# A two-stage transformer on one core: attention heads in another order, a bias mask on GpSimd, and other slots for VectorE's work

## The reference

```python
proj = rms_norm(x, pre_mix_norm[l]) @ w_in[l]
a_out = neighbourhood_attention(na_q, na_k, na_v, na_rel_bias[l])    # bias table and window mask
b_out = diff_attention(dq1, dq2, dk1, dk2, df_v, lam, alibi_slopes)  # 4 heads, two softmaxes each
b_out = rms_norm(b_out, diff_subln[l]) * (1.0 - lambda_init)         # norm over each head's 64 columns
c_out = gqa_attention(rope(norm(gq_q)), rope(norm(gq_k)), gq_v)
d_out = mla_attention(q_nope, q_rope, k_nope, k_rope, v)
x = x + rms_norm(concat(a_out, b_out, c_out, d_out) @ w_o[l], post_mix_norm[l])
x = x + rms_norm(ffn(rms_norm(x)), post_ffn_norm[l])                 # SwiGLU, 2816 wide
```

## Time and profile before

| what | value |
|---|---|
| time, median of 3 runs (lowest to highest) | 1947.78 us (1947.43 to 1951.02) |
| the profiled execution: its time, its span | 1951.02 us, 1949.2 us |
| TensorE busy, mean granted clock | 1883.7 us (97%), 0.989 |
| VectorE, ScalarE, GpSimd busy | 1343.0 us (69%), 995.4 us (51%), 68.5 us (4%) |
| shares of the chain that ended last | PE 81%, DVE 9%, ACT 4% |

### The profile page before, as it was taken

One profiled execution on the slowest core, in us unless ns is written; L12 is line 12 of the kernel. 1 busy time (PEld: TensorE's weight loads), 2 busy tenths in 40 slices (PEclk: granted clock), 3 DMA queues, 4 the chain that ended last, 5 costly groups with the idle time before them and its releaser, 6 DMA issues.

```text
span 1949.2 us, 34518 instructions
## 1 busy us (share of the span) xinstructions
PE 1883.7 (97%) x13470; PEld 1730.1 (89%) x13470; DVE 1343.0 (69%) x2141; ACT 995.4 (51%) x1534; POOL 68.5 (4%) x82
## 2 busy tenths in 40 slices
PE   8999999999999999999999999998999999999998
PEld 7978999898899987899989799998989998979997
DVE  5757888675788876788878578885555555665555
ACT  7755333765533466633374453346655335655333
POOL 3002000000000000000000000003300000000000
PEclk9999999999999999999999999999999999999999
DMA  8527988532788842588853368874335554325552
GB/s 288 191 90 238 359 311 311 185 130 89 286 316 314 310 149 94 212 323 311 314 193 130 132 247 322 313 292 171 141 114 200 183 185 171 111 85 179 188 194 86
DMA packets 60355, 412.22 MB, mean 211 GB/s; under 512 B 8592, under 2 KB 8784, under 8 KB 11616
## 3 DMA queue, kind: packets, MB, share of 16 engines
q1 hardware_dynamic: 55728, 401.33, 55.7%
q0 software_dynamic: 4528, 9.56, 1.8%
HBM read 409.71 MB, written 3.16 MB: 212 GB/s over the span
## 4 chain that ended last, share of the span: by engine, by line
PE 81%; DVE 9%; ACT 4%; DVEq 2%; issue 2%; ACTq 1%; DMA 0%; SPq 0%
PE psu L502 33%; PE psy L661 16%; PE psy L564 6%; PE psy L610 5%; PE psy L556 4%; PE psm L736 3%; PE psu L519 3%; PE psu L721 2%; DVE wlo L855 2%; PE psy L632 2%; PE psy L543 1%; PE pso L707 1%; DVE ada_raw L1017 1%; DVE x L1084 1%; ACT whi L846 1%
## 5 line engine op out<-in xcount | busy, mean ns | idle before, releaser
L846 ACT CAST whi<-raw 128x2048 fp32r<-128x2048 f32 (+1 forms) x281 | 536.2, 1908 | 624.6 <-PE psu L502 424.3
L855 DVE TENSOR_TENSOR wlo<-raw,whi 128x2048 fp32r<-128x2048 f32 (+5 forms) x296 | 645.4, 2181 | 276.4 <-ACT whi L846 275.0
L502 PE MATMUL psu<-hhi,whi 128*128 128x256 f32 x1920 | 537.0, 280 | 0.0
L502 PE MATMUL psu<-hlo,whi 128*128 128x256 f32 x1920 | 535.9, 279 | 0.0
L502 PE MATMUL psu<-hhi,wlo 128*128 128x256 f32 x1920 | 535.8, 279 | 0.0
L502 PEld LDWEIGHTS psu<-hhi,whi 128*128 128x128 f32 x1920 | 360.8, 188 | 3.0
L502 PEld LDWEIGHTS psu<-hlo,whi 128*128 128x128 f32 x1920 | 360.8, 188 | 2.4
L502 PEld LDWEIGHTS psu<-hhi,wlo 128*128 128x128 f32 x1920 | 360.8, 188 | 0.0
L1017 DVE CUSTOM_DVE_ANT_0 ada_raw<-ada_raw,cvec 128x1024 f32<-128x1024 f32 x192 | 227.0, 1219 | 1.3 <-DMA ada_raw<-ada 1.2
L661 PE MATMUL psy<-whi,ahi 128*128 128x512 f32 x528 | 210.5, 399 | 1.0 <-DVE alo L1036 0.9
L661 PE MATMUL psy<-wlo,ahi 128*128 128x512 f32 x528 | 208.0, 394 | 0.0
(11 more groups left out here) (342 smaller groups left out, 3055.2 us busy)
## 6 DMA issues: line engine op xcount, KB each, us to landing
raw<-wts SPq DMA_DIRECT2D x280, 1024.0 KB, 4.8
ada_raw<-ada SPq DMA_DIRECT2D x96, 1024.0 KB, 4.8
dense_bias<-rel_bias POOLq DMA_DIRECT2D x32, 64.0 KB, 12.5
nab<-dense_bias SPq DMA_DIRECT2D x2, 1024.0 KB, 7.6
ada_raw<-fox_rows POOLq DMA_DIRECT2D x4, 512.0 KB, 6.8
cb<-cst POOLq DMA_DIRECT2D x1, 1408.0 KB, 8.5
cb<-cst SPq DMA_DIRECT2D x1, 1056.0 KB, 10.6
x<-x_in SPq DMA_DIRECT2D x2, 512.0 KB, 4.7
```

Source lines behind the costliest of these rows:

```text
L502: last = mm(psu[:, bank, cc * SEQ:(cc + 1) * SEQ], a[:, cols], h[:, kt, :], start=(kt == 0 and j == 0), stop=(kt == KT - 1 and j == 2))
L846: nc.scalar.copy(whi[:, part_of(c), 0:n], raw[:, slot_of(c), 0:n]).then_inc(hi_done, 1)
L855: last = nc.vector.tensor_tensor(wlo[:, part_of(c), cols], raw[:, slot_of(c), cols], whi[:, part_of(c), cols].bitcast(f32), ALU.subtract)
```

## The change

1. MIX: the items' order is gqa, diff, na, mla. The result's columns, the rows of `w_o` and the turns are permuted to fit: turns 0 and 1 (gqa) go to slots 17 and 19, and turns 2 and 3 (diff) at 28 and 29 wait for `mix_ready`. `sub_sums` goes from slot 22 to 26, the square root with its table changes from 22 to 27, `sub_norm` from 23 to 27.
2. MIX: the queries' transposes for gqa go to the bank `psy[:, 2]` (was `psu[:, 1]`).
3. MIX: `neighbour_mask` is gone from VectorE; GpSimd adds the mask in one instruction over 128x2048, as soon as the bias table has landed. The na items wait for it (`na_ready`).
4. FOX: GpSimd adds the columns by eight `tensor_scalar` per group (four 128x128, four 128x256) with drains, in place of three `tensor_tensor` with a broadcast column.
5. GLA: the second half of the ada step goes from slot 40 to 7; `take_level(0)` from slot 16 to 17; the `dve_lo` that stood at slot 16 behind it is at slot 15. All other entries of `GLA.lo` stay as they were.

```diff
@@ -79,14 +79,13 @@
...
 MIX = Plan([2 if u is None else 4 for u in W_IN1], [3, 3, 2] + [2] * 11 + [1] * 20 + [2] * 4, range(12, 32),
-           [24, 25, 28, 29, 30, 31, 33, 35], "00 01 10 02 03 11 12 13",
+           [17, 19, 28, 29, 30, 31, 33, 35], "00 01 10 02 03 11 12 13",
            [2, 3, 5, 7, 10, 11, 13, 14, 18, 22, 26, 30, 34], 24)
...
            "00 01 10 02 03 11 12 13", [2, 4, 6, 8, 13, 17, 20, 24], 16)
-GLA = Plan([4] * 13, [3, 4, 1] + [1] * 60, [], [45, 46, 49, 50, 52, 53, 55, 57], "00 10 01 11 02 12 03 13",
-           [2, 3, 7, 11, 16] + list(range(19, 63, 4)))
+GLA = Plan([4] * 13, [3, 4, 1] + [1] * 60, [], [45, 46, 49, 50, 52, 53, 55, 57], "00 10 01 11 02 12 03 13")
 GLA_LEVEL = {16: 0, 18: 1, 22: 2, 26: 3, 30: 4, 34: 5, 38: 6}
...
@@ -242,6 +241,7 @@
...
+        na_ready = sem("na_ready")
...
@@ -282,7 +282,6 @@
...
-        fox_sum = sem("fox_sum")
...
@@ -455,6 +454,11 @@
...
                 pool.dma_start(gain[:], gain_mix[l].partition_broadcast(P)).then_inc(gain_loaded, 16)
+                pool.wait_ge(na_loaded, 16 * (l + 1))
+                pool.wait_ge(cb1_loaded, 16)
+                nb = fold(nab[:], 32, 64)
+                mask = cb[:, CB1["na"][0]:CB1["na"][1]]
+                nc.gpsimd.tensor_tensor(nb, nb, mask.unsqueeze(1).to_broadcast([P, 32, 64]), ALU.add).then_inc(na_ready, 1)
                 pool.wait_ge(x_ready, 8 + 8 * l)
...
@@ -475,11 +479,14 @@
...
                 first = fold(nab[:, g4 * 512:(g4 + 1) * 512], 4, P)
-                own, later = (lcq[:, at + 4 * g4:at + 4 * g4 + 4].unsqueeze(2).to_broadcast([P, 4, P]) for at in (0, 16))
-                nc.gpsimd.tensor_tensor(first, rows4[:, :, 0:P], own, ALU.add)
-                nc.gpsimd.tensor_tensor(rows4[:, :, P:], rows4[:, :, P:], later, ALU.add).then_inc(fox_sum, 1)
-                pool.wait_ge(fox_sum, g4 + 1)
-                nc.gpsimd.tensor_tensor(rows4[:, :, 0:P], rows4[:, :, 0:P], later, ALU.add)
+                for i in range(4):
+                    h = 4 * g4 + i
+                    nc.gpsimd.tensor_scalar(first[:, i], rows4[:, i, 0:P], lcq[:, h:h + 1], None, ALU.add)
+                nc.gpsimd.drain()
+                for i in range(4):
+                    h = 4 * g4 + i
+                    nc.gpsimd.tensor_scalar(rows4[:, i], rows4[:, i], lcq[:, 16 + h:17 + h], None, ALU.add)
+                nc.gpsimd.drain()
                 nc.gpsimd.tensor_tensor(first, first, mask, ALU.add)
...
@@ -750,10 +757,10 @@
...
             if m is not None:
-                if m < 2:
+                if m in (2, 3):
                     pe.wait_ge(mix_ready, l + 1)
                 else:
-                    pe.wait_ge(o_evac, I0 + 2 * m + 6)
+                    pe.wait_ge(o_evac, I0 + (2 * m + 2 if m < 2 else 2 * m + 6))
                 pe_turn(pe, l, m)
...
@@ -1116,26 +1123,26 @@
...
                                     [gv[:, kc * P + kv * HD:kc * P + (kv + 1) * HD] for kc in range(2)],
-                                    256 + (2 * c + kv) * HD, pre=(gqa_ready, l + 1), vpre=(bank_free, b0 + 4)))
+                                    (2 * c + kv) * HD, pre=(gqa_ready, l + 1), vpre=(bank_free, b0 + 4)))
             for h in range(4):
...
                                     [dfv[:, kc * 256 + h * HD:kc * 256 + (h + 1) * HD] for kc in range(2)],
-                                    h * HD, table=distance_table, slope=2.0 ** (-8.0 * (h + 1) / 4), pair=which,
+                                    256 + h * HD, table=distance_table, slope=2.0 ** (-8.0 * (h + 1) / 4), pair=which,
                                     pre=(bank_free, b0 + 6), vpre=(bank_free, b0 + 7)))
...
                                 [nav[:, kc * 256 + h * HD:kc * 256 + (h + 1) * HD] for kc in range(2)],
-                                512 + h * HD, table=na_table(h),
+                                512 + h * HD, table=na_table(h), tpre=(na_ready, l + 1),
                                 pre=(bank_free, b0 + 9), vpre=(bank_free, b0 + 10)))
...
                                 768 + h * HD, pre=(ml_cev, 4 * l + 4), vpre=(ml_evac, l + 1)))
-            return out[4:12] + out[0:4] + out[12:]
+            return out
 
...
@@ -1195,7 +1202,7 @@
...
                         for k in range(2):
-                            nc.tensor.transpose(psu[:, 1, k * SEQ + t * P:k * SEQ + (t + 1) * P],
+                            nc.tensor.transpose(psy[:, 2, k * SEQ + t * P:k * SEQ + (t + 1) * P],
                                                 gqr[:, t * 256 + k * P:t * 256 + (k + 1) * P], ident[:])
...
@@ -1279,13 +1286,13 @@
...
                     act.wait_ge(gq_tr, l + 1)
-                    nc.scalar.activation(gqT, psu[:, 1], ACT.Copy, scale=HD ** -0.5)
+                    nc.scalar.activation(gqT, psy[:, 2], ACT.Copy, scale=HD ** -0.5)
                     nc.scalar.copy(gkT, psy[:, 3, 0:SEQ]).then_inc(gqa_ready, 1)
...
                     nc.scalar.copy(to[0:96, h0 * SEQ:(h0 + 2) * SEQ], psy[0:96, 3]).then_inc(ml_cev, 1)
-                if h == 22:
+                if h == 27:
                     act.wait_ge(sub_sum, l + 1)
...
@@ -1371,7 +1378,7 @@
...
-            dh = rows[:, :, 0:256]
+            dh = rows[:, :, 256:512]
...
@@ -1390,13 +1397,6 @@
...
                                         ALU.mult).then_inc(mix_ready, 1)
-
-            def neighbour_mask(h0, n):
-                dve.wait_ge(na_loaded, 16 * (l + 1))
-                for h in range(h0, h0 + n):
-                    bias = fold(nab[:], NT, 4, 4, 64)[:, :, h]
-                    mask = cb[:, CB1["na"][0]:CB1["na"][1]].unsqueeze(1).unsqueeze(1).to_broadcast([P, NT, 4, 64])
-                    nc.vector.tensor_tensor(bias, bias, mask, ALU.add)
 
...
@@ -1414,14 +1414,9 @@
...
                     latent_rope()
-                if h == 19:
-                    neighbour_mask(0, 1)
-                if h == 21:
-                    neighbour_mask(1, 1)
-                if h == 22:
+                if h == 26:
                     sub_sums()
-                    neighbour_mask(2, 2)
-                if h == 23:
+                if h == 27:
                     sub_norm()
...
@@ -1892,8 +1887,8 @@
...
                     dve_turn(dve, GLA.turn[h], g, 0)
-                if h in (4, 40):
-                    dve_ada(dve, g, 0, h // 40)
+                if h in (4, 7):
+                    dve_ada(dve, g, 0, h // 7)
                 if h == 6:
...
@@ -1921,9 +1916,7 @@
...
                     nc.vector.tensor_tensor(g_D, g_D, g_kT, ALU.mult).then_inc(g_kd, 1)
-                if h == 16:
-                    take_level(0)
-                if GLA_LEVEL.get(h - 1, 0) >= 1:
+                if h - 1 in GLA_LEVEL:
                     nc.vector.drain()
...
@@ -2138,8 +2131,8 @@
...
-        w_o = a["w_o"][l].reshape(4, 256, D)[[1, 2, 0, 3]]
-        w_o[1] = w_o[1].reshape(4, HD, D)[[0, 2, 1, 3]].reshape(256, D)
+        w_o = a["w_o"][l].reshape(4, 256, D)[[2, 1, 0, 3]]
+        w_o[0] = w_o[0].reshape(4, HD, D)[[0, 2, 1, 3]].reshape(256, D)
...
```

## The result

| | us |
|---|---|
| changed kernel, median of 5 runs (lowest to highest) | 1965.42 (1963.86 to 1968.62) |
| kernel before, 5 runs beside it | 1947.50 |
| ratio, 95% interval | 1.0089 [1.0076, 1.0103] |
| predicted | 1953.8 (1946.5 to 1960) |

The sign was as forecast; the loss is 17.9 us and not 6. It lies above the range. Its busy times, from the page (against the earlier trace rows): GpSimd's rose by 24 us, TensorE's by 6.7 and its weight loads' by 6.1, the others' by less than 1.

A forecast was written before the change was run, and what follows sets the result against it. TensorE, busy 97% of the span, was taken as the bound. Terms -13.0 + 5.8 + 0.6 + 3.0 + 0.3 + 2.9 + 0 + 6.8 = +6.4, rounded to +6, gave 1953.8 us on the median of 1947.8; range 1946.5 to 1960.

The forecast's parts named there:

- 1. The old stall goes: MIX slots 22 to 25: TensorE's waits and the lower clock behind them vanish in both layers, -13.0 us.
- the queries' copies end ahead of the first scores: MIX, gqa's transposes in the other bank: copies out of it finish before the first scores, costing nothing.
- 2. The norm: MIX slots 26 to 28: the moved norm makes turn 2 wait 2.9 us per layer, 5.8 us in all.
- 3. The mask: MIX: GpSimd's long mask instruction holds up VectorE's split, 3.0 us in the second layer, 0.3 in the first.
- 4. GLA: GLA level 0: the earlier ada half and the split ahead of it delay VectorE, a TensorE stall of 2.9 us.
- 5. FOX at 0: FOX: the `tensor_scalar` additions on GpSimd fit within the time before VectorE's first use, 0 us.
- Plus drains: FOX: drains counted alongside five more instructions, within an extra of between nothing and 4 us that still fits.
- the bound of 4 us above: FOX: GpSimd's additions take at most 4 us more than 6.4, within the 10.7 us before VectorE's first use.
- FOX's tables come late: Rival, FOX: `tensor_scalar` takes twice the time per element, +4 us or more, 1958 and up; chance 0.10.
- 6. The clock: Behind four new stalls in MIX and GLA the lower clock costs 1.7 us each, 6.8 us in all.
- the clock stays up: Rival, whole kernel: no lower clock after single stalls, so -0.8 us, 1947; chance 0.12.

The follow-up runs named there:

- mix_order: The kernel before with the new MIX items' order, turns and norm alone: 1944.68 us, 0.9986 to before.
- u_mask: The changed kernel with the neighbourhood masks back on VectorE: 1953.95 us, 1.0029 to before.
- u_gla: The changed kernel with GLA's ada half, level 0 and weight split as before: 1962.72 us, 1.0079 to before.
- u_fox: The changed kernel with FOX's tables made as before (three `tensor_tensor` and a semaphore): 1959.23 us, 1.0049 to before.
- norm_early: mix_order with the square root one slot earlier, a weight split one slot later and two masks moved: 1937.69 us, 0.9947 to before.
- gla_lvl: The kernel before with only GLA's level 0 moved behind the weight split: 1948.29 us, 0.9997 to before.
- gla_ada: The kernel before with only GLA's second ada half moved from slot 40 to 7: 1947.86 us, 1.0000 to before.
- fox_sem: The kernel before with FOX's `tensor_scalar` form, but semaphore waits in place of the drains: 1947.46 us, 0.9998 to before.

## Why the prediction was wrong

| part | predicted, with its clock | measured |
|---|---|---|
| 1 and 2: old stall, norm, turns | -13.0 + 6.4 + 3.4 = -3.2 | -2.6 (mix_order) |
| 3: mask | 3.3 + 1.7 = +5.0 | +11.5 (u_mask) |
| 4: GLA | 2.9 + 1.7 = +4.6 | +2.7 (u_gla) |
| 5: FOX | 0 | +6.2 (u_fox) |
| sum | +6.4 | +17.8 |

The 11.4 us between the sums are 6.5 of the mask, 6.2 of FOX, 0.6 of MIX, less 1.9 of GLA.

**1. The old stall goes: right.** No wait stands at slots 22 to 24 with the mask on GpSimd; with the masks on VectorE, which the step did not treat, 0.7 is left. That the queries' copies end ahead of the first scores was wrong by the 0.60 us at slot 12, in the first layer alone. The bank is not the cause: the copy out of it took 0.64 us at 55.67, before it took 0.65 at 55.38. With gqa first, slot 12 has scores that need it.

**2. The norm: right.** It is 2.54 us in both layers, where 2.9 stood, by the chain as written; norm_early, which changes that chain, removed it. The clock took 1.7 each in the profiled execution, as taken, but that size was in part luck: behind the same 2.54 us in the second layer it took nothing in mix_order and 3.4 in u_mask.

**3. The mask: the second layer right, the first layer is a step that failed.** Less the offset of 5.7 us with which the changed kernel comes to the second layer, GpSimd began at 403.5 (403.6 was written) and the split at 405.6 (405.76). The instruction took 4.55 instead of 5.1, so the stall is 2.26 instead of 3.0. In the first layer I took the one landing of the earlier trace rows, 75.7, as fixed (its issue at 68.1 us turned out to be the latest of sixteen), and looked only at the split behind it. The ada pass of slot 16 began at 73.46 in that same trace, and I did not ask what happens if the table lands 2 us earlier. It did, at 73.4: 2.69 us and 3.4 of clock instead of 0.3. Mask together: 2.69 + 2.26 + 6.8 of clock, less 1.4 that VectorE's masks cost at slot 24, is 10.3, of 11.5 measured.

**4. GLA: the mechanism right, 2.28 instead of 2.9.** That ada and the split add up is shown by gla_lvl and gla_ada. With 1.7 of clock the profile has 4.0; u_gla gives 2.7, with an interval that holds both; as its executions may or may not have the first layer's stall of 6 us, its median says little on the size.

**5. FOX at 0: the step that failed.** The elements and the five instructions more were weighed rightly (fox_sem: no difference). "Plus drains" stood in the estimate without a price; the bound of 4 us above had no row behind it for them, and the first drain took 6.56 us. The rival "FOX's tables come late" had its place and price right (+4 or more, 1958 and up) but another cause, and 0.10.

**6. The clock: right as a mechanism, its size less than half.** 6.8 us were written for four stalls. The profile has 15.3 in six windows: two stalls more, and the mask's two and FOX's took 3.4 each and not 1.7. The 2.8 and 3.4 us per layer from which the step worked were themselves one draw: of the eight profiled executions with MIX as before (before and the FOX and GLA kernels made from it) three have 0.83 and not 0.66 in the first layer's window 100 to 110, behind the same old stall. So no run gives a fixed clock price for a stall, and the split of the 11.4 us between stalls and clock holds for the profiled execution only. The rival "the clock stays up" is out for the kernel as a whole.

## What to carry to other kernels

A GpSimd instruction that reads SBUF held up VectorE's instructions with two operands in SBUF for its whole length here, so cut it into pieces, and don't rely on which of the two starts first when a DMA decides it. Between dependent GpSimd instructions wait on a semaphore and not with a drain where GpSimd has DMAs of its own under way. Where a trace shows one time for an event that starts a new instruction, ask what lies within two microseconds on either side of it.

## What was not expected of the hardware

- A GpSimd drain waits for GpSimd's own outstanding DMAs: 5.5 us with four row loads under way, 17.3 us with four more, 1.09 with all landed, 0.17 later on.
- `tensor_scalar` on GpSimd took 0.60 us for 128x128 (the median of sixteen in fox_sem) and 0.91 for 128x256 (four in 3.63): half the elements for two thirds of the time, and not twice the time per element, as the rival on FOX had feared.
- Whichever of the two engines starts first holds the other off: 0.05 us decided whether VectorE lost 4.3 us or GpSimd 1.0.
- A stall of 2.2 to 2.7 us was followed by a window of granted clock 0.66 in some places and 0.83 in others, and by none after 2.54 in mix_order's second layer. One and the same stall, 2.7 us in the first layer, had 0.66 behind it in the changed kernel and 0.83 in u_fox: its length does not tell what the clock takes.
